# Block orders of the streamed operand in the feed-forward matmuls of a two-part transformer kernel

## The reference

```python
D_MODEL = 1024
SEQ = 512
D_FF = 2816

def swiglu_ffn(h, w_gate_up, w_down):
    gate, up = jnp.split(h @ w_gate_up, 2, axis=-1)
    return (jax.nn.silu(gate) * up) @ w_down

for layer in range(2):
    ...
    x = x + swiglu_ffn(rms_norm(x, ffn_norm[layer]), ffn_w_gate_up[layer], ffn_w_down[layer])
```

## The kernel before

| stage | turns x products | pieces of each | matmuls |
|---|---|---|---|
| gu0, gu1 (gate and up, layers 0 and 1) | 11 x 4 | 8 | 1056 each |
| dn0, dn1 (down) | 2 x 12 | 8, 7, 7 in turn | 528 each |

## Time and profile before

### The profile page before, as it was taken

How to read it: one execution, slowest core, us unless ns; L and a number is a source line. 1 busy time by engine, 2 the same in 40 slices (tenths; PEclk the granted TensorE clock), 3 DMA queues, 4 the chain that set the end, 5 groups by cost and what they waited for, 6 DMA issues and landing times.

```text
span 1848.7 us, 24262 instructions
## 1 busy us (share of the span) xinstructions
PE 1792.0 (97%) x8806; PEld 1380.2 (75%) x8806; DVE 1078.4 (58%) x1752; ACT 838.4 (45%) x1404; POOL 209.3 (11%) x293
## 2 busy tenths in 40 slices
PE   9889999999999999999999999999999999999997
PEld 6777878888887766678888888868766777866675
DVE  8883454444434767755444434466576676577656
ACT  5413344434223667644444322233467633256763
POOL 7980000000000000000000000023000202200010
PEclk9989999999999999999999999999999999999999
DMA  6322222222333111122222223323111122311111
GB/s 211 86 77 80 92 91 102 91 99 91 94 96 109 48 33 30 51 71 96 96 101 92 100 87 96 106 76 107 69 57 54 50 80 88 108 57 58 46 58 57
DMA packets 58766, 152.14 MB, mean 82 GB/s; under 512 B 17153, under 2 KB 22049, under 8 KB 58673
## 3 DMA queue, kind: packets, MB, share of 16 engines
q1 hardware_dynamic: 55120, 148.21, 23.9%
q0 software_dynamic: 3552, 2.70, 0.5%
HBM read 143.73 MB, written 4.19 MB: 80 GB/s over the span
## 4 chain that ended last, share of the span: by engine, by line
PE 85%; DVE 6%; ACT 4%; POOL 3%; issue 2%; DMA 0%; SPq 0%; DVEq 0%; ACTq 0%; POOLq 0%
PE bank L2067 18%; PE bank L2068 18%; PE bank L2069 18%; PE bank L2568 3%; PE bank L2570 3%; PE bank L2569 3%; PE bank L2521 2%; PE bank L2550 2%; PE bank L2551 2%; PE bank L2552 2%; PE bank L2294 1%; DVE wl L1275 1%; PE bank L2322 1%; PE bank L2583 1%; PE bank L2308 1%
## 5 line engine op out<-in xcount | busy, mean ns | idle before, releaser
L1275 DVE TENSOR_TENSOR wl<-raw,wh 128x1024 fp32r<-128x1024 f32 (+3 forms) x280 | 324.9, 1161 | 477.9 <-ACT wh L693 474.6
L693 ACT ACTIVATE wh<-raw 128x1024 fp32r<-128x1024 f32 (+3 forms) x280 | 279.2, 997 | 565.3 <-PE bank L2069 495.2
L2067 PE MATMUL bank<-xH,wh 128*128 128x512 f32 x872 | 342.5, 393 | 0.6 <-DVE wl L1275 0.6
L2069 PE MATMUL bank<-xH,wl 128*128 128x512 f32 x872 | 339.9, 390 | 0.0
L2068 PE MATMUL bank<-xL,wh 128*128 128x512 f32 x872 | 339.8, 390 | 0.0
L2067 PEld LDWEIGHTS bank<-xH,wh 128*128 128x128 f32 x872 | 163.9, 188 | 36.9 <-issue 2.9
L2068 PEld LDWEIGHTS bank<-xL,wh 128*128 128x128 f32 x872 | 164.0, 188 | 34.6 <-issue 1.0
L2069 PEld LDWEIGHTS bank<-xH,wl 128*128 128x128 f32 x872 | 163.9, 188 | 34.0
L2067 PE MATMUL bank<-hidH,wh 128*128 128x512 f32 x352 | 137.3, 390 | 0.0
L2068 PE MATMUL bank<-hidL,wh 128*128 128x512 f32 x352 | 137.0, 389 | 0.0
L2069 PE MATMUL bank<-hidH,wl 128*128 128x512 f32 x352 | 137.0, 389 | 0.0
(11 more groups left out here) (455 smaller groups left out, 3353.1 us busy)
## 6 DMA issues: line engine op xcount, KB each, us to landing
raw<-w_gu_dram SPq DMA_DIRECT2D x88, 512.0 KB, 3.2
raw<-w_p_dram SPq DMA_DIRECT2D x64, 512.0 KB, 3.2
raw<-w_dn_dram SPq DMA_DIRECT2D x32, 448.0 KB, 3.2
raw<-w_glu_dram SPq DMA_DIRECT2D x16, 512.0 KB, 3.3
raw<-w_dn_dram SPq DMA_DIRECT2D x16, 512.0 KB, 3.5
raw<-w_out_dram SPq DMA_DIRECT2D x16, 512.0 KB, 3.2
raw<-w_in_dram SPq DMA_DIRECT2D x8, 512.0 KB, 7.9
raw<-w_o_dram SPq DMA_DIRECT2D x8, 512.0 KB, 3.2
```

The source lines that it names most:

```text
L693: nc.scalar.activation(wh[:, (st.base + u) % 2, 0:kts * P], raw[:, (st.base + u) % 4, 0:kts * P], ACT.Copy).then_inc(w_high, 1)
L1275: nc.vector.tensor_tensor(wl[:, s, 0:kts * P], raw[:, (st.base + u) % 4, 0:kts * P], wh[:, s, 0:kts * P].bitcast(F32), ALU.subtract).then_ ...
L2067: nc.tensor.matmul(bank, wh[:, s, w], hi[:, k, :], start=first and kt == 0, stop=False)
L2069: ins = nc.tensor.matmul(bank, wl[:, s, w], hi[:, k, :], start=False, stop=last and kt == kts - 1)
```

## The change

`product` now passes all three matmuls a view of the moving operand and the same view of the output bank. Every column still meets its own output column; only the order in which the 512 columns are streamed and written is another one, and it depends on the stage:

| stage | view (blocks are of adjacent columns) | shape of the view | runs | steps to a column that is not the next one |
|---|---|---|---|---|
| gu0 | blocks of 64: the even ones, then the odd ones | 2 x 4 x 64 | 8 | 7 |
| dn0 | blocks of 16: every fourth from block 0, then from 1, 2, 3 | 4 x 8 x 16 | 32 | 31 |
| gu1 | blocks of 128: the last first | 4 x 128 | 4 | 3 |
| dn1 | blocks of 32: the even ones, then the odd ones | 2 x 8 x 32 | 16 | 15 |

All other stages call `product` with the operand as it is. The branch for the first product of gu0 and gu1 is left as it was, which leaves 1032 + 528 + 1032 + 528 = 3120 changed matmuls.

```diff
+    def in_blocks(st, a):
+
+        order = {"gu0": "p (c r b) -> p r c b", "dn0": "p (c r b) -> p r c b", "dn1": "p (c r b) -> p r c b"}.get(st.name)
+        if st.name == "gu1":
+            return a.rearrange("p (c b) -> p c b", b=P)[:, ::-1, :]
+        width = {"gu0": (2, 64), "dn0": (4, 16), "dn1": (2, 32)}.get(st.name)
+        return a.rearrange(order, r=width[0], b=width[1]) if order else a
...
-                    nc.tensor.matmul(bank, wh[:, s, w], hi[:, k, :], start=first and kt == 0, stop=False)
-                    nc.tensor.matmul(bank, wh[:, s, w], lo[:, k, :], start=False, stop=False)
-                    ins = nc.tensor.matmul(bank, wl[:, s, w], hi[:, k, :], start=False, stop=last and kt == kts - 1)
+                    to, high_in, low_in = (in_blocks(st, a) for a in (bank, hi[:, k, :], lo[:, k, :]))
+                    nc.tensor.matmul(to, wh[:, s, w], high_in, start=first and kt == 0, stop=False)
+                    nc.tensor.matmul(to, wh[:, s, w], low_in, start=False, stop=False)
+                    ins = nc.tensor.matmul(to, wl[:, s, w], high_in, start=False, stop=last and kt == kts - 1)
```

## The result

The changed kernel takes 1860.12 us (median of four runs, 1858.57 to 1860.99) against 1849.85 us for the kernel before, measured beside it. The ratio is 1.0056 with a 95% interval of 1.0044 to 1.0068. It is slower, clear of the 0.2% that a measurement can tell, and no change was forecast.

A forecast was written before the change was run, and what follows sets the result against it. TensorE, busy for 97% of the span, was taken to bound the kernel. The single term, 3120 changed matmuls x 0 ns, summed to 0, so the forecast was 1850.7 us, with a range of 1847.5 to 1866 us.

The forecast's parts named there:

- What bounds the kernel, and the lever: Four changed stages: TensorE's matmul pace lies on the path in full; one ns a matmul is 3.12 us.
- Reading in blocks: Moving-operand read: 34608 breaks at 0 to 0.07 ns make 0 to 2.4 us; taken as 0.
- the upper end of the next term: Writes in blocks: at most 0.20 us more a matmul, 624 us in all orders or 106 us in dn0 alone.
- Writing in blocks, and stepping backwards: Bank writes with breaks and gu1's descending order: 0 taken, between a gain of 41.8 us and a loss of 624 us.
- The pace does not depend on what addresses are read: Ground for taking 0: starts 0.22 to 0.23 us apart with `xH` and `hidH`; similar durations with weights as moving operand.
- a column time per break: Rival, bank or moving-operand addresses: each break costs one 2.4 GHz cycle, 14.4 us more, 1865 us; chance 0.13.
- Half pace writes: Rival, bank writes: short runs double dn0, 1957 us, or all four stages, 2474 us; within the 0.09 for larger slowdowns.
- the orders are not carried out: Rival, changed views: the program makes plain patterns of them again, 1850.7 us; chance 0.01, counted in no change.
- The 13.4 ns beyond the columns: Changed matmuls: what each takes of 226.7 ns beyond 213.3 ns for its 512 columns; at most 41.8 us in all.
- the faster rival: Changed matmuls: the order takes reads out of the weight load's way, up to 41.8 us back, 1808.6 us; chance 0.08.
- The likeliest case: Whole kernel: no change, with d, the order's cost per matmul, at 0; 1847.5 to 1854 us, chance 0.70.
- The rule on lines: Memory rule weighed: non-contiguous PSUM patterns slow matmuls, sum far above zero; neighbours sharing lines, sum zero, which the prediction followed.

The follow-up runs named there:

- the fifth experiment: Kernel before with some 64-column weight loads in gu0 (16-column blocks) and gu1 (plain), and plain float32 reads in dn0 (plain) and dn1 (16-column blocks): 2528.71 us.

## Why the prediction was wrong

**What bounds the kernel, and the lever:** right. TensorE's pace in the four stages is on the path in full; the 12.0 us added there reached the end, less the 4 us elsewhere in the one profile that go with the clock. No other engine's work changed: ACT's wait for TensorE stayed at 95.4 us in gu0 and grew in dn0 by about what TensorE lost, from 64.1 to 70.7.

**Reading in blocks:** this is the step that failed. It bounded the price of a break by the pair of lines 2163 and 2174 at 0 to 0.07 ns, 2.4 us in all, and argued that these matmuls read as many columns per ns as the changed ones. The number 2.34 counted records, and two matmuls of 64 output columns run side by side there. One such stream leaves two records of 110 ns (twice 54.8) for its 128 columns, 0.58 columns a ns and not 2.34, as the operands are plain float32. In that format short runs are free, which the float32 half of the fifth experiment shows directly at 429 ns with and without blocks. In fp32r the same blocks cost 12.8 ns (16 columns, dn0) and 9.9 ns (32 columns, dn1) a matmul, 12.0 us in all, where the prediction had 0. A row on another element format was taken for a row on the same read; what it is in the format that makes the read tolerant is not shown. In the upper end of the next term the same slip made a float32 matmul 0.43 us long instead of 0.86; nothing hung on it.

**Writing in blocks, and stepping backwards:** right at the value taken, 0. The write costs nothing down to pairs, and descending blocks of 128 and 64 cost nothing.

**"The pace does not depend on what addresses are read":** wrong, and it is the second support of the 0. The rows compared many addresses of one kind: the tiles of `xH` and `hidH` are 512 columns long, the weight pieces 128, and the kernel's regions begin at whole kilobytes from each other or are moved there by `start_level`, which counts modulo 512 bytes, so all of them start at the same place modulo 64 columns. A displacement by 16 or 32 columns would have shown 3 to 6 ns.

**The rivals.** The one that ended slower, a column time per break, has the sign and nearly the size (14.4 us against 12.0 in the stages and 10.3 by the medians), but its mechanism is wrong: it wanted 13, 2.9, 1.25 and 6.25 ns in dn0, gu0, gu1 and dn1, and the trace has 12.8, 0.0, 0.0 and 9.9. dn0 fits by chance, down to the 126.5 us forecast for its stage; gu0 and dn1 refute it. It was given 0.13. "Half pace writes" and "the orders are not carried out" did not happen. The 13.4 ns beyond the columns did react to the order, as the faster rival supposed, but only upwards.

**The numbers.** 1860.12 us lies inside the range only because that took in the band of the rival, 1854 to 1866, whose mechanism is wrong: that is luck. The likeliest case, with its chance of 0.70 and a d of 0, was wrong.

**The rule on lines.** The sentence of the Trainium skill on PSUM (Advanced Engine Details and Errata, section Memory Cachelines) would have given the right sign for a wrong reason. Its sentence on shared lines gave zero and was followed; the runs of 16 were four whole lines each, and still cost.

## What to carry to other kernels

The fp32r matmuls of this kernel, which stream one 4-byte column each cycle beside a weight load, ran at their best when the moving read and the weight read kept the same place modulo 256 bytes, which plain tiles on aligned starts do by themselves. When a view reorders or displaces such an operand, keep runs of 64 columns on multiples of 64; most else cost 1 to 6% of the matmul's time here, runs of 4 and 8 at far places up to 23%, and reads that skip parts of four columns up to twice the time. The write side took every order that was tried, down to pairs, for nothing, so a permutation belongs there. And before a row is used as the price of an access, check that it is a row on the same element format, and how many records one instruction leaves.

## What was not expected of the hardware

- A read without any break costs 232.7 to 233.0 ns instead of 226.7 when it starts 32 columns off, and the same when the weights are 32 off instead; both off together cost 227.7.
- 64 weight columns instead of 128 did not make the matmul beside them faster (228.6 to 230.8 ns). That the two reads must be in step is shown; by what they get in each other's way is not.
- Out of step, the price is not a function of width or breaks that these runs settle: 230.7 to 240.2 ns for most orders, 243 to 278 for runs of 4 and 8 at far places, 333 to 463 for single columns and pairs that are not read backwards. In dn0 single matmuls vary from 231 to 247 ns. This stays open.
- The order of the write was free in 13 forms of the experiments and the change, the narrowest of them pairs.
